# Four gate slabs beside the last dilated attention items, norm sums closed by one more matmul, and both directions of a linear attention interleaved

## The chip, the cores and the metric

One Trainium2 chip, one core. The metric is the device time of one execution in microseconds (us). The kernel is one program with five instruction streams: TensorE (PE), VectorE (DVE), ScalarE (ACT), GpSimd (POOL) and SyncE (SP, which only issues DMAs). They meet at semaphores.

## The reference, cut to what matters

Two transformer blocks run one after the other on 512 tokens of width 1024, with a context of 256 tokens beside the second. Everything is f32.

```
# first block
merged = sigmoid(gate_dn) * (o_dn @ w_branch_dn) + sigmoid(gate_da) * (o_da @ w_branch_da)
h = h + merged @ w_out            # o_dn: gated delta rule, o_da: dilated attention
# norm, used ten times
y = x * rsqrt(mean(x*x) + eps) * g
# linear attention (GLA) of the second block, for both directions
b = cumsum(log_sigmoid(z) / 16)                       # per chunk of 64 tokens
q_in, k_in, k_end = q * exp(b), k * exp(-b), k * exp(b_last - b)
a_intra = where(lower, q_in @ k_in.T, 0)
state_{c+1} = exp(b_last) * state_c + k_end.T @ v     # scan over the chunks
o = a_intra @ v + q_in @ state_c                      # then neighbourhood and window attention
```

The second block has two layers. Layer 0 runs the GLA for the context (c0) and for the latent tokens (l0), layer 1 needs only the context's final states (c1) and the latent tokens (l1).

## The kernel before, in words

**Slabs.** Each weight matrix is cut into slabs of 128 output features. A slab is loaded by SP into one of four raw buffers, split by ACT (`split_scalar`, L502) and DVE or POOL (`split_lower`, L510) into a high and a low part, and multiplied by TensorE in 24 matmuls of 512 columns (`unit_tensor`, L544, L546, L555): high by high, high by low, low by high. A slab of 512 tokens takes TensorE 5.44 us. The list `spine` fixes the order of all slabs.

**Side streams.** All work that is no slab (delta rule, dilated attention, GLA, attention) is written as generators, one for each engine. A planner (`Weave`) walks through the spine before the program is written, keeps a modelled clock for each engine, and puts the next step of a side stream between the matmuls of a slab when its model says that the operands will be there. What comes out is one static order for every engine. An engine that waits at the head of its order holds up all that was placed behind it. `drain` places the rest of a stream with no slab beside it.

**Dilated attention.** Four heads of four items each (`dilated_tensor`): scores (L1471 to L1473), softmax, six transposes (L1479), twelve matmuls with the values (L1491), a transpose back (L1497). The items of a head can start only after its last value slab. After the 36 slabs of the dilated projections come the four slabs z; then the stream is drained, the residual is loaded (`xres`, L1757), and the gates and merges follow.

**Norm sums.** ACT squares the eight blocks (`square_scalar`, L618), POOL adds the first seven (`sum_gpsimd`, L632), and TensorE sums over the partitions by a matmul with ones: one for POOL's sum (L638) and one for the eighth square (L640).

**GLA.** The generator `gla(m)` runs direction 0 from end to end and then direction 1. For each direction: decay matmuls (L1984) and their bias on DVE (L2152); Abs, Exp, Ln on ACT (L2085 to L2089); softplus, the two scans and the difference on DVE (L2156 to L2163); three or four Exp on ACT (L2096 to L2104); the products with keys and queries (L2169, L2173, L2238); key transposes (L2000); the states by chunk (L2013, mask L2183) and their scan (L2195); the entering states times the queries (L2031); scores inside the chunks and their product with the values (L2045, L2209, L2055). When direction 1 is done the event `mixed` lets the first lane of the neighbourhood attention begin; the output norm of the GLA (L2069, L2131 to L2139, L2218, L2221) gives the event `normed`, at which the second lane begins; a third lane begins after the last projection slab. In layer l the attention of 12 near items is then drained with what is left of the lanes, since the output slabs need its results. In the latent layers (`lat`), l0 stands for layer 0 and l1 for layer 1; 23 projection slabs run beside the GLA.

Of the kernel before, what the change touches and what calls it, by code (L numbers as in the profile page):

```python
# [15 lines left out]
T = 512  # L16
# [391 lines left out]
def program(nc, io):  # L408
# [215 lines left out]
    def sum_gpsimd(g, nm, use, c, before=None):  # L624
        g.wait_ge("sum_a", use, c)
        if c == 0:
            if before:
                g.wait_ge("sum_t", before)
            g.x.tensor_copy(nm.acc[:], nm.sq[0][:]).then_inc(*g.gives("sum_g", use, c))  # L629
        elif c < KC - 1:  # L630
            g.wait_ge("sum_g", use, c - 1)
            g.x.tensor_tensor(nm.acc[:], nm.acc[:], nm.sq[c % 2][:], ALU.add).then_inc(*g.gives("sum_g", use, c))  # L632

    def sum_tensor(t, nm, use):
        o = take(t, nm.ring, ("norm", use), ("norm_a", use, "ln"))[:, 0:nm.n]
# [4 lines left out]
        t.x.matmul(o, ones[:], nm.sq[(KC - 1) % 2][:], start=False, stop=True).then_inc(*t.gives("sum_t", use))  # L640
# [1058 lines left out]
    gate = [sb(f"gate{i}", WK + 82 + 2 * i, [T]) for i in range(6)]  # L1699
    mg_hi, mg_lo = sb("mg_hi", WK + 56, [KC, T], F32R), sb("mg_lo", WK + 98, [KC, T], F32R)  # L1700
    mg_pairs = [Pair(mg_hi[:, c], mg_lo[:, c], ("merge_a", c), ("merge_v", "lo", c)) for c in range(KC)]

    def gate_buffer(which, o):
        return gate[(2 * o + "dn da".split().index(which)) % 6]
# [91 lines left out]
    def ctxnorm_tensor(t):  # L1796
        for c in range(KC):
            yield 0.9
        yield coming("clate", ("sum_g", "c0mix", KC - 2), ("sum_a", "c0mix", KC - 1))
# [36 lines left out]
    class Mixer:  # L1836


        def __init__(self, name, l, v, n, base, full, pairs):
# [27 lines left out]
            self.dec = sb(f"{name}_dec", 8.5 if lat else 8.75, [2, self.NCH])  # L1867
# [79 lines left out]
    def gla(m):  # L1947
# [18 lines left out]

        def tensor(t):
            for i in range(2):
                yield When(("evac", place_of["proj", (m, "gv", i)], 0))
                yield coming(m.ring, m.there("gv", i))  # L1970
                b = take(t, m.ring, (name, "gv", i), ("gla_v", name, "gv", i))
                t.wait_ge(*m.there("gv", i))
                for o, s in zip(blocks(b), blocks(m.gvT[:, i])):
                    ins = t.x.transpose(o, s, ident)
                ins.then_inc(*t.gives("gla_t", name, "gv", i))
                yield 0.3
            yield When(("evac", place_of["proj", (m, "za", 0)], 0))
            for d in range(2):
# [8 lines left out]
                if d == 0:  # L1987
                    yield When(("evac", place_of["proj", (m, "gk", 1)], 0))
                    if full:
                        yield When(("evac", place_of["proj", (m, "gq", 1)], 0))  # L1990
                yield Ready(("gla_a", name, "soft", d))
                yield 0.3
                yield Ready(("gla_a", name, "past", d))
                yield 0.0
                yield coming(m.ring, ("gla_v", name, "kend", d), n=2)
# [7 lines left out]
                if d == 1 and full:  # L2003
                    yield Mark((name, "qk done"))
# [13 lines left out]
                if not full:  # L2018
                    continue
# [7 lines left out]
                for k, c in enumerate(chunks(d)):  # L2027
# [7 lines left out]
                    elif k % 2:  # L2035
                        yield 0.3
                for n0 in range(0, NT, 2):
# [22 lines left out]
                    yield 0.2  # L2060
            if not full:
# [13 lines left out]
        def scalar(a):  # L2075
            for i in range(2):
                yield
            for d in range(2):
                for i in range(2):
                    a.wait_ge("gla_v", name, "z", d, i)  # L2080
                if d:
                    a.wait_ge("gla_g", name, "kin", 0) if full else a.wait_ge("gla_v", name, "kend", 0)
                for f in m.idle:
                    a.wait_ge(*f)
                a.x.activation(m.C[:], m.tmp[:], ACT.Abs, bias=0.0, scale=1.0).then_inc(*a.gives("gla_a", name, "abs", d))  # L2085
                a.wait_ge("gla_a", name, "abs", d)
                a.x.activation(m.C[:], m.C[:], ACT.Exp, bias=0.0, scale=-1.0).then_inc(*a.gives("gla_a", name, "exp", d))
                a.wait_ge("gla_a", name, "exp", d)
                a.x.activation(m.C[:], m.C[:], ACT.Ln, bias=1.0, scale=1.0).then_inc(*a.gives("gla_a", name, "soft", d))  # L2089
                yield  # L2090
                C4 = m.C[:].rearrange("p i (c s) -> p i c s", s=64)
                for i in range(2):
                    a.wait_ge("gla_v", name, "scan", d, i)
                if d:
                    a.wait_ge("gla_v", name, "state", 0, NCH - 1, 1)
                a.x.activation(m.dec[:], C4[:, :, :, 63 if d == 0 else 0], ACT.Exp, bias=0.0, scale=-1.0 / 16).then_inc(  # L2096
                    *a.gives("gla_a", name, "dec", d))
                a.wait_ge("gla_v", name, "past", d)
                a.x.activation(m.tmp[:], m.tmp[:], ACT.Exp, bias=0.0, scale=1.0 / 16).then_inc(*a.gives("gla_a", name, "past", d))
                if full:  # L2100
                    if d:
                        a.wait_ge("gla_t", name, "mix", 0, NT - 2)
                    a.x.activation(m.kin[:], m.C[:], ACT.Exp, bias=0.0, scale=1.0 / 16).then_inc(*a.gives("gla_a", name, "kin", d))
                    a.x.activation(m.qin[:], m.C[:], ACT.Exp, bias=0.0, scale=-1.0 / 16).then_inc(*a.gives("gla_a", name, "qin", d))  # L2104
                yield
                yield
# [7 lines left out]
                for _ in groups:  # L2114
                    yield
                if full:
                    for k in range(NCH - 1):
                        if k % 2:
                            yield
                    for n0 in range(0, NT, 2):  # L2120
                        yield
                        yield
# [18 lines left out]
        def vector(v):  # L2141
            for i in range(2):
                v.wait_ge("gla_t", name, "gv", i)
# [2041 lines left out]
```

## Time and profile before

| | us |
|---|---|
| median of 3 runs | 4046.06 (4045.66 to 4049.22) |
| the profiled execution | 4052.06 |
| its span, first to last instruction | 4049.8 |
| TensorE busy in the span | 3809.7 |
| mean granted clock of TensorE, as a share of full speed | 0.971 |

A row of the timeline has the start, the length, the engine, the line of the kernel, the operation with out<-in, the number of instructions merged, and in square brackets the time that the engine sat idle before it and who released it. A row of the windows has the stretch, its length, busy time and number of instructions of PE, PE's weight loads, DVE, ACT and POOL, then the granted clock, the DMA share and GB/s.

### The profile page before, as it was taken

The page shows a single profiled execution, that of the slowest core. Times are in us where ns is not written, and L with a number is a line of the kernel's source. Part 1 is how long each engine was busy: PE and PEld are TensorE (multiplying, and loading weights), DVE is VectorE, ACT ScalarE, POOL GpSimd, SP SyncE. Part 2 cuts the span into 40 slices and gives each one's busy share as a digit, 9 for nine tenths or more (in the row PEclk, how much of TensorE's full clock was granted, in tenths as well). Part 3 has the DMA queues.
Part 4 walks back from the last instruction along what each step waited for, and adds up shares of the span by engine and source line. Part 5 has one row for each costly group of instructions (what it writes and reads, how often), then busy time and mean ns, then how long its engine had stood idle before and what let it go on. Part 6 is the DMA issues. An engine that isn't in the chain of part 4 may idle for free. (4 is left out here: it accounts for less than half of the span.)

```text
span 4049.8 us, 57241 instructions
## 1 busy us (share of the span) xinstructions
PE 3809.7 (94%) x23037; PEld 3306.3 (82%) x23037; DVE 2407.7 (59%) x4212; ACT 1633.0 (40%) x2618; POOL 789.6 (19%) x630
## 2 busy tenths in 40 slices
PE   8999989989897989999999999997999999789998
PEld 5787767677797879999999999775687877677887
DVE  6455332456899777777777777556643335664333
ACT  4523332344455763333333333526532234564222
POOL 0112000253215643222332221201000010101000
PEclk9999999999999999999999999998999999899999
DMA  5211334432354479888888886321234332102322
GB/s 206 68 44 43 106 125 177 169 106 86 107 170 156 171 249 309 275 289 273 285 274 294 275 288 210 113 67 49 71 119 140 125 135 79 60 30 83 99 94 78
DMA packets 209191, 617.28 MB, mean 152 GB/s; under 512 B 18464, under 2 KB 68640, under 8 KB 205088
## 3 DMA queue, kind: packets, MB, share of 16 engines
q1 hardware_dynamic: 168352, 465.76, 34.7%
q0 software_dynamic: 40576, 147.87, 10.3%
q8 instruction: 183, 3.00, 0.3%
q14 instruction: 80, 0.66, 0.0%
HBM read 583.67 MB, written 29.88 MB: 152 GB/s over the span
## 5 line engine op out<-in xcount | busy, mean ns | idle before, releaser
L510 DVE TENSOR_TENSOR wlo<-raw,whi 128x1024 fp32r<-128x1024 f32 x576 | 714.6, 1241 | 676.0 <-ACT whi L502 668.2
L544 PE MATMUL ps<-hhi,whi 128*128 128x512 f32 (+1 forms) x2824 | 1074.9, 381 | 13.2 <-ACT uact L3384 8.9
L546 PE MATMUL ps<-hlo,whi 128*128 128x512 f32 (+1 forms) x2824 | 1049.0, 371 | 0.4 <-DVE hlo L2609 0.4
L502 ACT ACTIVATE whi<-raw 128x1024 fp32r<-128x1024 f32 x660 | 694.7, 1054 | 622.1 <-PE ps L555 471.1
L555 PE MATMUL ps<-hhi,wlo 128*128 128x512 f32 (+1 forms) x2824 | 663.2, 373 | 0.0
L544 PEld LDWEIGHTS ps<-hhi,whi 128*128 128x128 f32 x2824 | 533.0, 189 | 116.2 <-issue 24.4
L546 PEld LDWEIGHTS ps<-hlo,whi 128*128 128x128 f32 x2824 | 533.2, 189 | 68.7 <-issue 3.6
L555 PEld LDWEIGHTS ps<-hhi,wlo 128*128 128x128 f32 x2824 | 511.4, 188 | 72.0 <-issue 4.8
L544 PE MATMUL ps<-ag_hi,whi 128*128 128x384 f32 x1024 | 342.1, 334 | 0.0
L546 PE MATMUL ps<-ag_lo,whi 128*128 128x384 f32 x1024 | 342.0, 334 | 0.0
L510 POOL TENSOR_TENSOR wlo<-raw,whi 128x1024 fp32r<-128x1024 f32 x85 | 210.4, 2484 | 184.2 <-ACT whi L502 183.5
L3500 POOL DMA_INDIRECT fetched<-peer_v_rows,rows x128 | 150.9, 1179 | 361.6 <-DVE xtok L3472 335.5
L3500 POOL DMA_INDIRECT fetched<-peer_u_rows,rows x128 | 153.3, 1198 | 338.5 <-DVE ract L3458 329.8
L3384 ACT ACTIVATE uact<-ps 128x384 f32<-128x384 f32 x128 | 63.0, 492 | 367.0 <-PE ps L555 367.0
L544 PE MATMUL ps<-hchi,whi 128*128 128x256 f32 x672 | 177.6, 298 | 33.3 <-ACT whi L502 21.4
L555 PE MATMUL ps<-ag_hi,wlo 128*128 128x384 f32 x1024 | 198.1, 334 | 0.0
L544 PEld LDWEIGHTS ps<-ag_hi,whi 128*128 128x128 f32 x1024 | 192.2, 188 | 0.0
L546 PEld LDWEIGHTS ps<-ag_lo,whi 128*128 128x128 f32 x1024 | 192.1, 188 | 0.0
L555 PEld LDWEIGHTS ps<-ag_hi,wlo 128*128 128x128 f32 x1024 | 179.4, 188 | 0.0
L546 PE MATMUL ps<-hclo,whi 128*128 128x256 f32 x672 | 172.3, 290 | 0.0
L3401 DVE TENSOR_TENSOR uact<-uact,gin 128x384 f32<-128x384 f32 x128 | 71.3, 557 | 163.9 <-ACT uact L3384 153.4
L629 POOL COPY nacc<-nsq 128x512 f32<-128x512 f32 x6 | 3.7, 610 | 820.6 <-ACT nsq L618 820.6
(630 smaller groups left out, 6303.3 us busy)
## 6 DMA issues: line engine op xcount, KB each, us to landing
raw<-w_in SPq DMA_DIRECT2D x151, 512.0 KB, 3.6
raw<-peer_u SPq DMA_DIRECT2D x128, 512.0 KB, 4.7
raw<-peer_v SPq DMA_DIRECT2D x128, 512.0 KB, 4.3
raw<-w_mod SPq DMA_DIRECT2D x96, 512.0 KB, 3.6
raw<-w_gate SPq DMA_DIRECT2D x66, 512.0 KB, 3.5
raw<-w_up SPq DMA_DIRECT2D x66, 512.0 KB, 3.5
raw<-w_down SPq DMA_DIRECT2D x66, 512.0 KB, 3.5
gate_dram<-stage SPq DMA_DIRECT2D x24, 1024.0 KB, 6.1
```

What stands on the lines that cost most here:

```text
L502: a.x.activation(whi[n % NW][:], raw[i % NRAW][:], ACT.Copy, bias=0.0, scale=1.0).then_inc(*a.gives("hi", i))
L510: e.x.tensor_tensor(wlo[n % NW][:], raw[i % NRAW][:], whi[n % NW][:].bitcast(F32), ALU.subtract).then_inc(*e.gives(*lo_sig(i)))
L544: t.x.matmul(o, w, p.hi, start=grp.opens and k == 0, stop=False)
L546: t.x.matmul(o, w, p.lo, start=False, stop=False)
L555: ins = t.x.matmul(o, lo[:, 128 * (starts[gi] + k):128 * (starts[gi] + k) + 128], p.hi, start=False, stop=grp.closes and k == len(grp.pair ...
L629: g.x.tensor_copy(nm.acc[:], nm.sq[0][:]).then_inc(*g.gives("sum_g", use, c))
L3384: a.x.activation(uact[j % 2][:], held(("out", "peer_u", j))[:, 0:TD], ACT.Gelu_apprx_tanh, bias=0.0, scale=1.0).then_inc(*a.gives("peer_a" ...
L3401: v.x.tensor_tensor(t3, t3, gin[g % 2][:, :, jj, :], ALU.mult).then_inc(*v.gives("peer_v", "gated", j))
L3500: g.x.indirect_dma_start(fetched[i % NF][:], None, io["peer_v_rows" if i >= 128 else "peer_u_rows"], bass.IndirectOffsetOnAxis(ap=rows[:, ...
```

## The change

Three edits. (1) The gate slabs dn and da of the first two output blocks stand before the z slabs instead of behind them. They get four buffers of their own, and their sigmoid waits for the last transpose of the delta rule's output. The spine runs eight slabs instead of four before the dilated stream is drained. (2) POOL adds six squares instead of seven; TensorE adds the seventh and the eighth by matmuls with ones. (3) `gla` is cut into named steps, and one order sets them for both directions: direction 1's decays, scans and key transposes are placed among the states and the entering part of direction 0. Direction 1 has its own decay buffer and works in the buffer of the value projections, free by then. The products of direction 1 with its queries and inner keys are still behind the mixing of direction 0.

```diff
-        elif c < KC - 1:
+        elif c < KC - 2:
             g.wait_ge("sum_g", use, c - 1)
             g.x.tensor_tensor(nm.acc[:], nm.acc[:], nm.sq[c % 2][:], ALU.add)...
-        t.wait_ge("sum_g", use, KC - 2)
+        t.wait_ge("sum_g", use, KC - 3)
         t.x.matmul(o, ones[:], nm.acc[:], start=True, stop=False)
-        t.wait_ge("sum_a", use, KC - 1)
-        t.x.matmul(o, ones[:], nm.sq[(KC - 1) % 2][:], start=False, stop=True)...
+        for c in (KC - 2, KC - 1):
+            t.wait_ge("sum_a", use, c)
+            ins = t.x.matmul(o, ones[:], nm.sq[c % 2][:], start=False, stop=c == KC - 1)
...
+    gate_first = [sb(f"gate_first{i}", WK + kb, [T]) for i, kb in enumerate((62, 64, 66, 60))]
...
-        if o >= 3:
+        if o < 2:
+            a.wait_ge("unit_t", 3)
+        elif o < 5:
+            a.wait_ge("da_v", "oda", 3, 3)
+        else:
             a.wait_ge("merge_v", "lo" if which == "dn" else "sum", o - 3)
-        else:
-            a.wait_ge("da_v", "oda", 3, 3)
...
+        decs, Cs = [m.dec, m.dec2], [m.C, m.gvT]
+        def order(values_by_token, gates, decays, ends, turning, sums, entered, mix, keys):
+            yield from values_by_token()
+            yield from gates(0)
+            yield from decays(0)
+            yield from keys(0)
+            yield from ends(0)
+            yield from turning(0)
+            yield from gates(1)
+            yield from sums(0)
+            yield from decays(1)
+            if full:
+                yield from entered(0)
+            yield from ends(1)
+            yield from turning(1)
+            if full:
+                yield from mix(0)
+            yield from keys(1)
+            yield from sums(1)
+            if full:
+                yield from entered(1)
+                yield from mix(1)
...
+                    if d and full and (c0, p) == groups[1]:
+                        queries(d)
...
-    spine += ... + coupled(u_da[-12:], m0[16:32]) + u_z + u_merge[:2]
-    spine += coupled(u_merge[2:] + u_out[:6], m0[32:] + m1[:16]) + u_out[6:]
+    spine += ... + coupled(u_da[-12:], m0[16:32]) + u_merge[:4] + u_z
+    spine += coupled(u_merge[4:] + u_out[:6], m0[32:] + m1[:16]) + u_out[6:]
...
     run(36)
-    run(4)
+    run(8)
     plan.drain("dilated")
     plan.put("do", "xres")
-    run(24)
+    run(20)
```

In the named steps, `gates` are the decay matmuls with Abs, Exp, Ln; `decays` softplus, scans and Exp; `keys` the two Exp for inner keys and queries; `ends` the product with the keys; `turning` the key transposes; `sums` the states and their scan; `entered` and `mix` the two parts of the output.

## Rows read from the trace of the kernel before

**Rows 1.** The page, part 1, TensorE.

```profile
PE 3809.7 (94%) x23037; PEld 3306.3 (82%) x23037; DVE 2407.7 (59%) x4212; ACT 1633.0 (40%) x2618; POOL 789.6 (19%) x630
```

**Rows 2.** Windows over the drained dilated items and the two latent layers.

```profile
577.00:598.00 21.00, 11.67 (x45) 8.94 (x45) 4.03 (x11) 7.66 (x12) 0.54 (x1) 0.59 0.35 119
2705.00:2750.00 45.00, 44.99 (x261) 36.43 (x260) 22.93 (x45) 18.26 (x28) 1.79 (x3) 1.00 0.15 48
2750.00:2800.00 50.00, 28.79 (x174) 20.12 (x173) 36.45 (x80) 33.22 (x65) 10.78 (x13) 0.69 0.21 67
2800.00:2830.00 30.00, 25.76 (x228) 20.39 (x224) 19.78 (x60) 18.50 (x40) 2.17 (x3) 0.90 0.09 28
3491.00:3541.00 50.00, 28.65 (x174) 19.90 (x172) 36.46 (x80) 33.16 (x65) 10.77 (x13) 0.68 0.21 67
3541.00:3571.00 30.00, 25.70 (x226) 20.47 (x226) 19.85 (x60) 18.50 (x40) 2.17 (x3) 0.90 0.09 27
```

**Rows 3.** Timeline of TensorE: scores of three dilated items, and the first gate slab.

```profile
560.97 1.02 PE L1471 MATMUL ps<-dk,dq 128*128 128x512 f32 x2
...
574.45 1.02 PE L1471 MATMUL ps<-dk,dq 128*128 128x512 f32 x2
...
587.09 2.07 PE L1471 MATMUL ps<-dk,dq 128*128 128x512 f32 x2 [0.47 <-DVE oda L1553]
...
597.99 0.47 PE L544 MATMUL ps<-hhi,whi 128*128 128x512 f32 x1
```

**Rows 4.** Timeline of ACT: one of six table loads between 550 and 588 us.

```profile
552.68 1.28 ACT L1590 ACT_TABLE_LOAD   x1
```

**Rows 5.** Timeline of SP: the loads of the residual.

```profile
580.89 3.65 SPq L1757 DMA_DIRECT2D xres<-xT  x8
```

**Rows 6.** Timeline of TensorE at two of the ten norm sums.

```profile
2927.27 1.13 PE L638 MATMUL ps<-nacc,ones 128*128 128x512 f32 x2 [1.19 <-POOL nacc L632]
...
3310.95 1.13 PE L640 MATMUL ps<-nsq,ones 128*128 128x512 f32 x2 [0.65 <-ACT nsq L618]
```

**Rows 7.** Timeline of TensorE: the GLA of l0, from the mixing of direction 0.

```profile
2664.41 1.09 PE L2055 MATMUL ps<-l_aT,l_gvtok 128*64 128x128 f32 x16
...
2692.23 1.03 PE L2000 MATMUL ps<-cst,l_tmp 128*128 128x128 f32 x8
...
2695.49 1.16 PE L2013 MATMUL ps<-l_gvtok,l_ktok 64*128 64x128 f32 x8
...
2711.11 0.55 PE L2031 MATMUL ps<-l_qin,l_S 128*128 128x64 f32 x4
...
2727.01 1.09 PE L2055 MATMUL ps<-l_aT,l_gvtok 128*64 128x128 f32 x16
```

**Rows 8.** Timeline of DVE in l0: scans of direction 1, end of the output norm.

```profile
2680.21 2.34 DVE L2160 TENSOR_TENSOR_SCAN l_C<-c,l_tmp 128x512 f32<-128x512 f32 x2
...
2747.02 0.75 DVE L2221 SCALAR_TENSOR_TENSOR l_tmp<-l_tmp,cst,l_gg 128x512 f32<-128x512 f32 x1
```

**Rows 9.** Timeline of ACT in l0: an Exp of direction 1.

```profile
2684.06 1.04 ACT L2099 ACTIVATE l_tmp<-l_tmp 128x1024 f32<-128x1024 f32 x1
```

**Rows 10.** Timeline of TensorE: near items of l0, and one item's transposes at full clock.

```profile
2735.59 0.36 PE L2396 MATMUL ps<-l_nks,l_nqd 128*128 128x256 f32 x1
...
2750.28 0.28 PE L2396 MATMUL ps<-l_nks,l_nqd 128*128 128x256 f32 x1
...
2761.92 0.55 PE L2396 MATMUL ps<-l_nks,l_nqd 128*128 128x256 f32 x1 [4.72 <-ACT l_nqd L2755]
...
2772.29 1.04 PE L2414 MATMUL ps<-cst,l_NS 128*128 128x128 f32 x8
...
2783.83 0.58 PE L2396 MATMUL ps<-l_nks,l_nqd 128*128 128x256 f32 x1 [5.35 <-DVE l_o L2515]
```

**Rows 11.** Timeline of TensorE: the longest GLA stalls of c0 and c1.

```profile
908.62 1.12 PE L2031 MATMUL ps<-c_qin,c_Sen 128*128 128x64 f32 x4 [2.76 <-DVE c_Sen L2195]
...
1432.01 0.63 PE L2000 MATMUL ps<-cst,c_tmp 128*128 128x128 f32 x4 [2.21 <-DVE c_tmp L2169]
```

More of the change, by code:

```diff
@@ L636, in sum_tensor @@
         t.wait_ge("ones_g")
-        t.wait_ge("sum_g", use, KC - 2)
+        t.wait_ge("sum_g", use, KC - 3)
         t.x.matmul(o, ones[:], nm.acc[:], start=True, stop=False)
-        t.wait_ge("sum_a", use, KC - 1)
-        t.x.matmul(o, ones[:], nm.sq[(KC - 1) % 2][:], start=False, stop=True).then_inc(*t.gives("sum_t", use))
+        for c in (KC - 2, KC - 1):
+            t.wait_ge("sum_a", use, c)
+            ins = t.x.matmul(o, ones[:], nm.sq[c % 2][:], start=False, stop=c == KC - 1)
+        ins.then_inc(*t.gives("sum_t", use))
     def root_scalar(a, nm, use, before=None, eps=EPS):
@@ L1703, in gate_buffer @@
     def gate_buffer(which, o):
-        return gate[(2 * o + "dn da".split().index(which)) % 6]
+        i = 2 * o + "dn da".split().index(which)
+        return gate[i % 6] if o >= 2 else gate_first[i]
     def gate_scalar(a, i, phase):
@@ new lines, in nothing, with steps, values_by_token, gates @@
+        def nothing(count):
+            def steps(*_):
+                for _ in range(count):
+                    yield
+            return steps
+        no_steps = {"values_by_token": nothing(2), "gates": nothing(1), "decays": nothing(1), "keys": nothing(0), "ends": nothing(1),
+                    "turning": nothing(1), "sums": nothing(len(groups)), "entered": nothing((NCH - 1) // 2), "mix": nothing(NT)}
+        def tensor(t):
+            def values_by_token():
+                for i in range(2):
+                    yield When(("evac", place_of["proj", (m, "gv", i)], 0))
+                    yield coming(m.ring, m.there("gv", i))
+                    b = take(t, m.ring, (name, "gv", i), ("gla_v", name, "gv", i))
+                    t.wait_ge(*m.there("gv", i))
+                    for o, s in zip(blocks(b), blocks(m.gvT[:, i])):
+                        ins = t.x.transpose(o, s, ident)
+                    ins.then_inc(*t.gives("gla_t", name, "gv", i))
+                    yield 0.3
+                yield When(("evac", place_of["proj", (m, "za", 0)], 0))
+            def gates(d):
@@ L2002, in tensor, with sums @@
                 yield 0.3
-                if d == 1 and full:
-                    yield Mark((name, "qk done"))
+            def sums(d):
                 for c0, p in groups:
@@ L2017, in tensor, with entered @@
                     yield 0.3
-                if not full:
-                    continue
+                if d == 1 and full:
+                    yield Mark((name, "qk done"))
+            def entered(d):
                 yield Ready(("gla_v", name, "qin", d), ("gla_v", name, "state", d, NCH - 2, 1),
@@ L2060, in tensor @@
                     yield 0.2
+            yield from order(**{**no_steps, "values_by_token": values_by_token, "gates": gates, "decays": decays, "ends": ends,
+                                "turning": turning, "sums": sums, "entered": entered, "mix": mix})
             if not full:
@@ L2113, in scalar @@
                 yield
[L2114 to L2122, printed above, removed]
+            yield from order(**{**no_steps, "gates": gates, "decays": decays, "keys": keys, "turning": turning})
             if not full:
@@ L2166, in vector, with ends @@
                 yield
+            def ends(d):
                 v.wait_ge("gla_a", name, "past", d)
@@ L2169, in vector, with queries, sums @@
                 v.x.tensor_tensor(m.tmp[:], m.tmp[:], m.gk[:], ALU.mult).then_inc(*v.gives("gla_v", name, "kend", d))
-                if full:
-                    v.wait_ge("gla_a", name, "qin", d)
-                    v.wait_ge(*m.there("gq", 1))
-                    v.x.tensor_tensor(m.qin[:], m.qin[:], m.gq[:], ALU.mult).then_inc(*v.gives("gla_v", name, "qin", d))
+                if full and d == 0:
+                    queries(d)
                 yield
-                yield
+            def queries(d):
+                v.wait_ge("gla_a", name, "qin", d)
+                v.wait_ge(*m.there("gq", 1))
+                v.x.tensor_tensor(m.qin[:], m.qin[:], m.gq[:], ALU.mult).then_inc(*v.gives("gla_v", name, "qin", d))
+            def sums(d):
                 if d:
@@ L2212, in vector @@
                     yield
+            yield from order(**{**no_steps, "values_by_token": values_by_token, "gates": gates, "decays": decays, "ends": ends,
+                                "sums": sums, "mix": mix})
             if not full:
@@ L2249, in gpsimd @@
                     g.x.tensor_copy(m.r_S[:, d], m.Sen[:, chunks(d)[-1]]).then_inc(*g.gives("gla_g", name, "final", d))
-                if not full:
-                    continue
-                for k in range(NCH - 1):
-                    if k % 2:
-                        yield
-                for n0 in range(0, NT, 2):
-                    yield
-                    yield
+            yield from order(**{**no_steps, "ends": ends, "sums": sums})
             if full:
```

109 lines of the change are left out of this document (52 added, 57 removed).

## The prediction, on record before the result was known

> **What bounds the kernel now.** I read the page first. TensorE is busy in 94% of the span [rows 1], so 4049.8 - 3809.7 = 240 us are all that waiting costs, beside what a lowered clock costs (mean clock 0.971). No edit here takes work off TensorE, and the second adds some. So a part of the change is worth what it removes of TensorE's idle time and of its time at the lower clock, and nothing else. The next view was the windows, over the whole span in slices of 50 us, to see where that time lies; three of the lowest stretches are next to the change [rows 2]. Between 577 and 598 us TensorE is busy for 11.67 us of 21, and the granted clock is 0.59: the reader is to see that even the busy time is stretched, since most of it runs at 1.2 GHz and not at 2.4. Behind each of the two latent layers' projections lie 80 us with 54.6 us busy at clocks of 0.69 and 0.90 (l0) and 54.4 us at 0.68 and 0.90 (l1). The 45 us before them are full: 44.99 us busy at 1.00. Last I read the timeline engine by engine in these stretches, to see what TensorE waits for and what had to come first.
>
> **The gate slabs.** The drained part of the dilated stream holds the end of one item and two whole ones, with scores at 574.45 and 587.09, and the first slab behind it starts at 597.99 [rows 3]. The work that TensorE has there is, at full clock, between 11.67 / 2 = 5.8 us (all of it was at half clock) and 11.67 x 0.59 = 6.9 us (busy time by mean clock) [rows 2]. So the stretch of 21 us loses 14.1 to 15.2 us. Four gate slabs, at 5.44 us each, are 21.8 us of TensorE work that is ready: they read only the normalised input. That is more than the hole. With cover, two items start 574.45 - 560.97 = 13.5 us apart [rows 3]. The item at 574.45 is the third of its head, so the first stands two of these steps ahead, near 548; four items need 3 x 13.5 from there and some 11 us to the end: 600. Eight slabs are 43.5 us, and with some 13 us of dilated work between them TensorE is full until about 605. The stream ends before the slabs do, and the whole loss goes: I take 14.5 us.
>
> Three things are queued anew. ACT changes its table for Sigmoid, Silu and Exp in turn; before, it did so six times in this part, at 1.28 us each [rows 4]. The new order has four more evacuations between the same four softmaxes, so at most two loads for each item, 2.6 us, of which an item had 1.28 or 2.56 before; the slack is (605 - 600) / 4 = 1.25 us an item, so it about fits. The residual's eight loads took 3.65 us to issue at 580.89, while TensorE waited anyway [rows 5]; now they are issued once z is gated, near 609, and the slab loads queued on SP stand behind them. Two slabs are split ahead and four more lie in the raw buffers, at least 11 us of work against about 4 us to wait and 4 us to issue, plus the bytes; I take 0, and 3 us as the bad end. The sigmoid waits for the delta rule's output, whose last part was done before 515 us by its place in the timeline: 0.
>
> The Trainium skill, in "ScalarE: Activation LUTs", "What ACT_TABLE_LOAD costs", gives about 1283 ns for a load and another 1380 ns of drain, 2.66 us for every switch, and in "Table sets: the hidden batching unit" asks for all work of one set before the next. It speaks against this edit, which mixes three sets. The trace agrees with the load (1.28 us) but shows no drain beside it: the activation behind the load of 552.68 starts as it ends, at 553.97. By the page's figure two switches an item would be 5.3 us, some 4 us over the pitch that I use, and the estimate for the gain would fall from 14.5 to 7 us.
>
> **The norm sums.** An extra matmul of 512 columns in f32 costs some 0.87 us at full clock (a pair of records starts about that far apart). Where POOL's last addition was waited for (1.19 us before L638 at 2927.27) the acc matmul can start 1.2 us sooner and is followed by one more: 1.19 - 0.87 = 0.3 us won, in l0 and again in l1. Where POOL was early and the last square came late (0.65 us before L640 at 3310.95) the extra matmul fills that wait and sticks out by 0.2 us; three sums look so [rows 6]. In the other five the sum lies beside slabs, at a low clock or behind a wait for ACT that stays. Together -0.3 us; both ends +-2 us.
>
> **The GLA.** In l0 direction 0 ends its mixing at 2665.5. Direction 1's key transposes come at 2692.23, its first states at 2695.49: 30 us in which only decays, scans and keys were made [rows 7]. In the new order these lie beside the states of direction 0. From the states on, direction 1 keeps what it had, 2695.49 to 2728.1. What is new before direction 0's mixing is a chain behind its state scan: softplus, two scans (2.34 us) and a difference, 4.8 us on DVE [rows 8]; a table load and an Exp of 1.04 us [rows 9]; the key product, 1.2 us; transposes (1.03 us) and their copy, 1.1 us. That is 11.5 us, of which the entering part hides 6 us: +5.5 us. The two Exp of `keys`(1) and the query product hide behind the first two state groups (2 x 2.2 us). So `mixed` comes 30 - 5.5 = 24 us earlier, at 2704 instead of 2728. TensorE's own work there is unchanged and was under full slabs, so this alone gives nothing. What counts is that the near attention starts under the slabs. Its first scores followed `mixed` by 7.5 us (2735.59); the second lane followed the end of the output norm (2747.8, 19.7 us after `mixed`) with scores at 2750.28 [rows 8, 10]. Now these come at 2711 and 2726, and the slabs, which ended at 2750, run to about 2762 because the attention's matmuls come between them. In the before, an item under slabs was slow: from 2735.59 its values were done near 2766, since its queue positions on DVE lay behind the output norm. Two lanes in 50 and 36 us get through 4 items by that measure (2 if each takes the 30 us seen, 6 if 14 us).
>
> The 80 us behind the slabs lose 80 - (28.79 x 0.69 + 25.76 x 0.90) = 37 us in l0 and the same in l1 [rows 2], for twelve items: 3.1 us an item. Four items fewer save 12.4 us. The stall of 4.72 us for the second set of operands [rows 10] goes too, since these follow the output norm and now fall under the slabs, and the 1.8 us of value copies beside it. Sum 18.9; I take 18 us a layer, 36 us for both. The bounds are 6 us a layer (two items, no stall gone: the like of the 5.35 us [rows 10] comes in its place) and 30 us (six items and both stalls). DVE has room for it: 22.93 us busy in the 45 us before [rows 2].
>
> In c0 the context attention begins only after the last slab, and TensorE is full there; in c1 the gate work of the experts follows at its own pace. An earlier GLA releases nobody. The stalls inside it, 2.76 and 2.21 us [rows 11], may go or be doubled by the new queue positions: I take -1 us, ends -5 and +5 us.
>
> **The sum.** 4052.06 - 14.5 - 0.3 - 36 - 1 = 4000.3 for an execution like the profiled one, which lies 2.3 us above its span and 6.0 us above the median of the runs. Against the median: 4046.06 - 51.8 = 3994 us.
>
> **The rivals.**
> (a) The near attention does not profit: earlier lanes sit behind other instructions in DVE's or ACT's fixed order, as the first item did for 30 us, and only as much as 0 to 4 us a layer is won. For it: that first item, and the third lane still waits for the last slab. Against: DVE is half idle there. Time 4046 - 15 - 4 = 4027.
> (b) The dilated items become slower than 14.75 us apart, by table loads or by the longer queue on ACT, and half or all of the first gain goes: 4001 to 4008.
> (c) The near attention gets nearly all of its 37 us back in both layers (six items or more and no new stall): 4046 - 15 - 66 - 3 = 3962.
> (d) The change moves the waits but not the end, all three parts: the slabs' order or the drains are bound by something that the profile puts down to another releaser: 4046.
> (e) On the other side: direction 1's decay steps stand early in the order of ACT and DVE, in front of slab splits. If TensorE runs out of split slabs (there are two, 10.9 us) because ACT waits there for DVE and DVE for the transposes, each latent layer and c0 pays 5.44 us or more and the attention behind it is not covered better. It decides from a loss of 14.5 / 2 = 7.3 us a layer on; at 12 us a layer the time is 4046 - 15 + 24 = 4055. Against: the same steps stood in the same queues before without a stall in 44.99 of 45 us.
>
> **How the numbers follow.** Forecast 0.62 (3966 to 4022), a 0.13, b 0.08, c 0.06, d 0.05, e 0.06. The low end is 4046 - 16 - 60 - 4 = 3966. The high end takes in a, with a bad end of the residual's loads and of c0: 4033. Outside are c in part, d and e, and together with the tail of a they are under 0.2. Within 0.2%, or 8 us, two times of this kernel can't be told apart. Faster by more than that: forecast, a, b, c, 0.89. Within: d, 0.05. Slower: e, 0.06.
>
> **What would show it.** Right: no idle hole of TensorE before `xres`, and 20 us less between the first z or gate slab and the first merge; the last L2055 of l0 some 24 us closer to its first L1974; near scores (L2396) for three or four items more before the last projection slab; less than 60 us from that slab to the last near item. Wrong: new idle time before L544 with whi as releaser in the GLA stages, or an unchanged distance from the last projection slab to the window attention.

## The result, and the profile after

The kernel after takes 4029.0 us (median of 5 runs, 4023.9 to 4035.6) against 4046.3 us: the ratio is 0.9956, 95% interval 0.9941 to 0.9970, so 17 us less and not the 52 us forecast. The profiled execution, the slowest of the five, has a span of 4033.8 us, 16.0 us under the 4049.8 us of before. Part 1 of its page:

```profile
PE 3813.2 (95%) x23057; PEld 3313.6 (82%) x23057; DVE 2406.4 (60%) x4212; ACT 1638.7 (41%) x2622; POOL 773.9 (19%) x620
```

**Where the 16 us come from.** The sums of the ten norms cut both programs at the same places. Between them the kernel after wins 9.2 us in the dilated stage, gate, merge and output slabs, 10.6 us in c0 with the context's attention, 1.5 us in l0 and 1.4 us in l1 (forecast 18 each); it loses 3.7 us between the context's two norms and 3 us in the stages not named here. The table of stages below has them for all kernels.

**Dilated items.** Windows of the kernel after, where [rows 2] has 577 to 598 us of before:

```profile
577.00:604.00 27.00, 27.00 (x140) 22.49 (x139) 10.93 (x20) 16.41 (x23) 0.54 (x1) 1.00 0.18 54
...
604.00:617.00 13.00, 8.84 (x42) 5.38 (x40) 2.04 (x3) 3.14 (x5) 0.00 (x0) 0.97 0.69 243
617.00:640.00 23.00, 21.96 (x92) 14.92 (x92) 6.86 (x8) 5.46 (x6) 0.00 (x0) 0.87 0.52 182
```

The hole is gone: 27.00 us busy of 27.00, clock 1.00. The next two rows are new: 4.16 + 1.04 us idle, and a mean clock of 0.87 in the second. That mean is 6.8 us at half clock (1.2 GHz) and full clock behind:

```profile
616.11:622.94 6.83, 4.90 (x11) 2.62 (x12) 2.45 (x2) 2.11 (x2) 0.00 (x0) 0.50 0.81 291
622.94:640.00 17.06, 17.06 (x82) 12.30 (x81) 4.41 (x6) 3.35 (x4) 0.00 (x0) 1.00 0.43 151
```

Timelines of TensorE and SP in the kernel after:

```profile
617.50 1.92 PE L827 MATMUL ps<-raw,svec 128*32 128x512 f32 x4 [4.66 <-DMA raw<-w_mod]
```

```profile
588.83 0.33 SPq L494 DMA_DIRECT2D raw<-w_mod  x1
606.64 3.65 SPq L1763 DMA_DIRECT2D xres<-xT  x8
610.33 0.46 SPq L494 DMA_DIRECT2D raw<-w_mod  x1
```

Between 588.83 and 610.33 SP issues no slab load: it stands at the residual's loads, which wait until z is gated, and TensorE runs out of loaded slabs.

**The latent layers.** TensorE in l0, kernel after. In [rows 7], counted from the first decay matmuls at 2598.43, direction 0 ended its mixing at 67.1 us and direction 1 at 129.7.

```profile
2582.69 1.10 PE L2026 MATMUL ps<-l_za,wa 128*128 128x512 f32 x2 [1.03 <-DVE l_gvtok L2195]
2615.68 1.36 PE L2048 MATMUL ps<-cst,l_tmp 128*128 128x128 f32 x8 [2.08 <-DVE l_tmp L2226]
2636.68 1.16 PE L2061 MATMUL ps<-l_gvtok,l_ktok 64*128 64x128 f32 x8
2649.19 0.50 PE L544 MATMUL ps<-hhi,whi 128*128 128x512 f32 x1 [2.12 <-DVE l_nk L1936]
2658.18 1.03 PE L2048 MATMUL ps<-cst,l_tmp 128*128 128x128 f32 x8
2670.50 1.09 PE L2107 MATMUL ps<-l_aT,l_gvtok 128*64 128x128 f32 x16
2672.65 1.16 PE L2061 MATMUL ps<-l_gvtok,l_ktok 64*128 64x128 f32 x8
2702.70 1.09 PE L2107 MATMUL ps<-l_aT,l_gvtok 128*64 128x128 f32 x16
2709.76 0.28 PE L2453 MATMUL ps<-l_nks,l_nqd 128*128 128x256 f32 x1
2714.99 0.86 PE L2764 MATMUL ps<-cst,l_nvT 128*128 128x128 f32 x4 [2.23 <-ACT l_C L2181]
2723.92 0.28 PE L2453 MATMUL ps<-l_nks,l_nqd 128*128 128x256 f32 x1
```

Counted from 2582.69, direction 0's last mixing (2670.50) ends at 88.9 us: 21.8 us later than before, where the prediction had 5.5. Direction 1's ends at 121.1: its part shrank from 62.6 to 32.2 us, as forecast, so `mixed` is 8.6 us earlier and not 24. And there are three waits of 2.1 to 2.2 us that were not there. Within 1.3 us behind each begins a stretch of 3.4 us at half clock; all the rest of the slab stretch is at full clock:

```profile
2616.32:2619.73 3.41, 3.41 (x11) 2.83 (x10) 1.49 (x2) 1.20 (x2) 0.00 (x0) 0.50 0.25 52
2650.45:2653.86 3.41, 3.41 (x14) 3.02 (x14) 2.71 (x3) 1.55 (x2) 0.00 (x0) 0.50 0.17 34
2715.30:2718.71 3.41, 3.41 (x14) 2.83 (x12) 0.85 (x2) 3.38 (x4) 0.00 (x0) 0.50 0.00 0
```

Windows of l0, the slab stretch from the first decay matmuls and the drained stretch behind it, first before, then after:

```profile
2598.40:2750.40 152.00, 150.38 (x794) 119.80 (x794) 78.51 (x115) 59.19 (x74) 8.48 (x9) 1.00 0.23 77
2750.40:2828.50 78.10, 52.65 (x389) 39.04 (x387) 55.72 (x138) 50.69 (x103) 12.95 (x16) 0.76 0.16 53
```

```profile
2582.70:2755.60 172.90, 165.90 (x878) 131.14 (x878) 99.96 (x159) 76.12 (x106) 15.80 (x17) 0.97 0.25 77
2755.60:2811.20 55.60, 36.21 (x303) 28.98 (x303) 37.27 (x95) 35.15 (x72) 5.82 (x8) 0.82 0.15 47
```

The drained stretch shrinks by 22.5 us, the slab stretch grows by 20.9. Of the 192 near value matmuls, all drained before, 32 (two items of twelve) now lie under the slabs, and the scores of two more items.

To weigh this, the loss is TensorE's idle time plus busy time times (1 - clock), summed over slices of 10 us. In l0, in us as idle + clock, for the slab stretch, the drained stretch and what follows up to the norm behind the attention:

| kernel | slabs | drained | to the norm |
|---|---|---|---|
| before | 1.6 + 0.0 | 25.4 + 11.2 | 7.1 + 0.0 |
| after | 7.0 + 4.1 | 19.4 + 5.2 | 5.9 + 1.4 |
| after, again | 7.2 + 1.3 | 19.4 + 3.7 | 5.8 + 2.9 |
| gates behind states | 6.0 + 2.7 | 16.2 + 6.4 | 5.8 + 0.0 |
| mixing first | 4.9 + 3.0 | 19.4 + 4.6 | 5.9 + 2.9 |
| GpSimd waits | 5.1 + 0.0 | 19.4 + 3.6 | 5.9 + 0.0 |
| three repairs | 3.9 + 1.7 | 16.8 + 6.7 | 5.8 + 1.4 |

The earlier attention saves 12.0 us of the drained loss (36.6 to 24.6), and the slab stretch gives 9.5 of it back (1.6 to 11.1).

### The profile page after: what moved, and what is told of

Same layout as the page of the kernel before. It is cut to its first block, busy times and chain, and to the rows that moved or that the text cites. A ratio compares the mean times of both kernels' runs of the same rounds, so it can differ in the third digit from the quotient of the medians.

```text
span 4033.8 us, 57266 instructions
## 1 busy us (share of the span) xinstructions
PE 3813.2 (95%) x23057; PEld 3313.6 (82%) x23057; DVE 2406.4 (60%) x4212; ACT 1638.7 (41%) x2622; POOL 773.9 (19%) x620
## 3 DMA queue, kind: packets, MB, share of 16 engines
q0 software_dynamic: 40576, 147.87, 10.4%
## 4 chain that ended last, share of the span: by engine, by line
PE 79%; DVE 11%; ACT 5%; DMA 2%; issue 2%; POOL 0%; SPq 0%; DVEq 0%; ACTq 0%; POOLq 0%
PE ps L544 22%; PE ps L546 21%; PE ps L555 21%; PE ps L2480 1%; PE ps L2453 1%; DMA raw<-w_in 1%; ACT whi L502 1%; PE ps L2471 1%; PE ps L827 1%; DVE hlo_plain L704 1%; PE ps L3351 1%; PE ps L2061 1%; DVE wlo L510 1%; DVE ea L3369 1%; DVE eb L3370 1%
```

## The experiments

Length of five stages in the profiled executions, in us: from the scores of the last head's first dilated item to the first latent norm sum; to the next context norm (c0 and its attention); to the one after; l0 and l1, each from the norm ahead of its projections to the norm behind its attention. The last columns are the median and the ratio to the kernel before, run beside each on its chip, with its interval.

| kernel | dilated to out | c0 | context | l0 | l1 | median | ratio |
|---|---|---|---|---|---|---|---|
| before | 258.0 | 280.1 | 289.2 | 354.2 | 359.4 | 4046.3 | 1 |
| after | 248.8 | 269.5 | 292.9 | 352.7 | 358.0 | 4029.0 | 0.9956 (0.9941, 0.9970) |
| gate slabs alone | 248.0 | 279.4 | 289.1 | 354.2 | 357.6 | 4040.0 | 0.9983 (0.9973, 0.9992) |
| norm sums alone | 257.0 | 278.0 | 292.3 | 353.1 | 357.6 | 4048.9 | 1.0002 (0.9993, 1.0011) |
| GLA order alone | 256.6 | 269.8 | 287.8 | 353.9 | 359.4 | 4039.9 | 0.9982 (0.9973, 0.9991) |
| after, old order in l0, l1 | 248.0 | 268.8 | 293.1 | 353.2 | 357.7 | 4034.4 | 0.9965 (0.9951, 0.9978) |
| residual later | 241.3 | 268.8 | 291.6 | 352.2 | 358.1 | 4021.5 | 0.9934 (0.9920, 0.9947) |
| mixing first | 249.1 | 268.3 | 291.7 | 348.6 | 353.8 | 4023.3 | 0.9936 (0.9922, 0.9950) |
| gates behind states | 251.3 | 268.8 | 291.8 | 347.0 | 353.3 | 4025.2 | 0.9941 (0.9927, 0.9955) |
| mixing first, all | 249.5 | 269.8 | 292.6 | 348.6 | 353.8 | 4025.9 | 0.9937 (0.9923, 0.9950) |
| after, again | 248.0 | 267.5 | 291.1 | 349.4 | 355.1 | 4030.4 | 0.9950 (0.9937, 0.9964) |
| GpSimd waits | 252.0 | 269.0 | 291.7 | 343.3 | 351.4 | 4025.1 | 0.9935 (0.9921, 0.9948) |
| two repairs | 240.9 | 268.8 | 291.8 | 347.0 | 353.3 | 4013.9 | 0.9907 (0.9891, 0.9922) |
| three repairs | 240.9 | 268.9 | 291.8 | 343.8 | 349.5 | 4007.9 | 0.9889 (0.9874, 0.9904) |

**Gate slabs alone.** Of the diff only the order of the slabs, their buffers and `run(8)`:

```diff
-    run(4)
+    run(8)
     plan.drain("dilated")
     plan.put("do", "xres")
```

> Only the four gate slabs ahead of the z slabs; norm sums and GLA as before. Theory A (read from the profile after): the hole of the drained dilated items goes (-14 us), but the residual's eight loads now stand ahead of the slab loads on SP until z is gated, TensorE waits about 5 us for a raw buffer near 617 us and runs some 3 us of work at a lower clock behind it; 8 us are left: 4038 us, with that wait in the trace. Rival B (the prediction's term, 14.5 us, is right and the loss of 5 us at 617 comes only together with the other edits): 4031.5 us, no wait for raw above 1 us near 617. Rival C: all 16 to 17 us of the change are this edit: 4029 us.

7 us by the ratio, 10.0 us in its stage, and the wait for raw is there (4.17 us at 614.60). Theory A; B's clean 14.5 us are not there, and C is out. The stage alone is a rough measure: it takes 248.0 to 252.0 us in the eight profiles that have this edit (and the residual's loads where they were), 256.6 to 258.0 us in the three that have not.

**Norm sums alone.**

```diff
-        elif c < KC - 1:
+        elif c < KC - 2:
```

> Only the seventh square summed by TensorE. Theory A: it moves waits and no time: 2.7 us won at the context norm near 1086 us (the wait for POOL's sum was 7.13 us), 3 us lost at the paired norms near 2567 us, where TensorE waits for two squares of ACT instead of one; others within 0.5 us each: 4046 us, within 2 us. Rival B: the prediction's 0.3 us with no such pair of larger terms: the same total, but the wait near 1086 us is still about 7 us.

No change, as both said, and by A's larger terms. Timeline of TensorE before, at the context norm and at the paired norms (two sums close together, near 2570 us):

```profile
1086.50 1.19 PE L638 MATMUL ps<-cnacc,ones 128*128 128x256 f32 x2 [7.13 <-POOL cnacc L632]
...
2567.76 2.04 PE L638 MATMUL ps<-chacc,ones 128*128 128x512 f32 x2 [3.96 <-POOL chacc L632]
2571.20 2.08 PE L640 MATMUL ps<-chsq,ones 128*128 128x512 f32 x2 [1.39 <-ACT chsq L618]
```

and with the norm edit alone:

```profile
1083.85 1.19 PE L638 MATMUL ps<-cnacc,ones 128*128 128x256 f32 x2 [4.41 <-POOL cnacc L632]
...
2565.91 1.12 PE L641 MATMUL ps<-chsq,ones 128*128 128x512 f32 x2 [1.69 <-ACT chsq L618]
2569.92 1.73 PE L641 MATMUL ps<-chsq,ones 128*128 128x512 f32 x2 [2.89 <-ACT chsq L618]
```

POOL's wait shrinks by 2.7 us at 1086, but the stage behind it grows by 3.1, and the first slab behind that norm starts at 1091.72 where it started at 1091.90; at the paired norms the wait of 3.96 us for POOL is gone, and two squares of ACT are waited for instead of one. The edit moved the wait from POOL to ACT.

**GLA order alone.**

```diff
+            yield from gates(1)
+            yield from sums(0)
+            yield from decays(1)
...
+            yield from ends(1)
+            yield from turning(1)
+            if full:
+                yield from mix(0)
```

> Only the new order of the two directions, in c0, c1, l0 and l1. Theory A (from the profile after): c0 gives 8 us, c1 nothing, each latent layer only 1.5 us, since direction 0's mixing ends 22 us later instead of 5.5: 4035 us. Rival B (the prediction): 18 us a latent layer and 1 us in the contexts: 4009 us. Rival C: the latent layers lose as much as c0 gives: 4046 us.

7 us by the ratio. c0 wins 10.3 us (280.1 to 269.8), l0 and l1 together 0.3. The long stage with c1 and the experts, which the table leaves out, grows from 1192.1 to 1196.0 us, mostly by the clock: in its first 200 us TensorE's idle time grows by 0.5 us only. Nearest to Theory A, with less from the latent layers, a loss with c1, and 4040 us instead of 4035. In c0 the order removed waits; before it had these in the timeline of TensorE, and this window:

```profile
859.82 0.39 PE L544 MATMUL ps<-hchi,whi 128*128 128x256 f32 x1 [3.49 <-ACT c_gg L1913]
889.52 0.38 PE L544 MATMUL ps<-hchi,whi 128*128 128x256 f32 x1 [1.43 <-ACT c_nvT L1913]
896.95 0.39 PE L544 MATMUL ps<-hchi,whi 128*128 128x256 f32 x1 [1.41 <-ACT c_res L1913]
```

```profile
900.00:945.00 45.00, 42.24 (x293) 38.64 (x292) 19.61 (x52) 17.31 (x28) 27.84 (x16) 0.92 0.42 129
```

and with the GLA order alone two waits and this window of the same slabs:

```profile
857.34 0.39 PE L544 MATMUL ps<-hchi,whi 128*128 128x256 f32 x1 [1.29 <-ACT c_gg L1914]
879.03 0.66 PE L2042 MATMUL ps<-cst,c_tmp 128*128 128x128 f32 x4 [1.66 <-DVE c_tmp L2220]
```

```profile
899.00:935.00 36.00, 36.00 (x266) 33.54 (x265) 11.93 (x43) 17.22 (x27) 23.66 (x11) 1.00 0.44 135
```

All of TensorE's waits from 800 to 1092 us fall from 32.6 to 26.9 us in sum, the 2.76 us of [rows 11] among them. Over nine windows of the stage the clock costs 4 to 5 us less: busy time at 0.92 became busy time at 1.00.

**The kernel after with the old order in l0 and l1.**

```diff
+    def gla(m):
+        return gla_new(m) if not m.lat else gla_old(m)
```

> The kernel after, with the old order of the GLA in l0 and l1 alone (c0 and c1 keep the new one). Theory A: the new order is worth 1.5 us in each latent layer, so taking it back costs 3 us against the kernel after: about 4032 us; the distance from the norm before l0 to the one before its feed-forward part grows by 1 to 2 us. Rival B (the prediction's 18 us a layer are there, and something else in the kernel after eats them): 4065 us. Rival C (the order costs time in the latent layers and the single profile hides it): under 4027 us.

The stages l0 and l1 are 353.2 and 357.7 us, within a microsecond of the first profile of the kernel after and 6.4 us in sum above its second one. By the ratios (0.9965 against 0.9956 and 0.9950) the old order costs 4 to 6 us, near Theory A's 3, but the intervals overlap, and l0 and l1 grew as A expected only against the second profile. The new order is worth 0 to 6 us for both layers; B's 36 us are out, C too.

**Residual later.**

```diff
     run(8)
     plan.drain("dilated")
+    run(6)
     plan.put("do", "xres")
-    run(20)
+    run(14)
```

> The kernel after with the residual's loads put behind six more slabs of the spine. Theory A: what eats the gate slabs' gain is the SP queue, on which the slab loads stand behind a wait for z; without it the wait for raw of 4.7 us near 617 us and the 3 us of low clock behind it go: 6 to 8 us faster than the kernel after, 4022 us. Rival B (the raw buffers themselves come free late, the residual's place does not matter): the wait stays, 4029 us. Rival C (the eight loads collide further on with slabs or are late for the first output slab): the wait turns up elsewhere between 640 and 800 us, 4029 us or more.

The stage falls from 248.8 to 241.3 us, no wait for raw is left, and the window behind the dilated items is full at full clock:

```profile
617.00:640.00 23.00, 23.00 (x108) 17.20 (x107) 7.15 (x8) 6.12 (x8) 0.00 (x0) 1.00 0.61 213
```

Theory A. With this the gate slabs give 16.7 us in their stage (258.0 to 241.3).

**Mixing first.** In l0 and l1:

```diff
-            yield from gates(1)
             yield from sums(0)
-            yield from decays(1)
+            yield from gates(1)
             if full:
                 yield from entered(0)
-            yield from ends(1)
-            yield from turning(1)
+            yield from decays(1)
             if full:
                 yield from mix(0)
+            yield from ends(1)
+            yield from turning(1)
```

> The kernel after; in l0 and l1 alone direction 1's gates come behind direction 0's states and its key product and transposes behind direction 0's mixing. Theory A (mixing of direction 0 was late because direction 1's gates, decays and transposes stood in front of it in every queue): the mixing of direction 0 ends 67 to 72 us after the first decay matmuls (89 in the kernel after), that of direction 1 at 100 to 106 us (121), two or three near items more lie under the slabs at 3 us each: 6 us a layer, 4017 us. Rival B (near attention under the slabs gives nothing, since what the drained stretch loses less the slab stretch loses more in waits and clock): direction 1 ends as early, the time is 4029 us. Rival C (the tail of direction 1 grows, since its decays have less cover): mixing of direction 1 at 115 us or later, 4029 us.

Direction 0's mixing ends at 80.5 us (not 67 to 72), direction 1's at 117.3 (not 100 to 106). As a mechanism A fell and C held: the head wins 8.4 us and the tail behind it gives 4.6 of them back. The time is not C's: l0 and l1 win 4.1 and 4.2 us against the first profile of the kernel after, 2.1 in sum against the second. The slab stretch loses 7.9 us instead of 11.1 (8.5 in the second profile). The median is 6 us lower than the kernel after's, and the intervals of the ratios overlap.

**Gates behind states.** In l0 and l1 only `gates(1)` and `sums(0)` change places.

> The kernel after; in l0 and l1 alone the gates of direction 1 come behind the states of direction 0 instead of ahead of them, all else as in the kernel after. Theory A: of the 22 us by which direction 0's mixing was late, the gates ahead of the states make 10 (seen at the end of the states: 54 us after the first decay matmuls instead of 43) and the decays and transposes ahead of the mixing the other 12; but Abs, Exp and Ln now lie behind the states and the decays wait for them, so the second part grows: direction 1's mixing ends 115 to 121 us after the first decay matmuls, time 4025 to 4029 us. Rival B: all 22 us come from the gates: direction 0's mixing back at 67 us, direction 1's near 100, 4017 us.

The states of direction 0 are back (the last group at 45.0 us instead of 54.0), its mixing ends at 86.8, direction 1's at 119.9. Theory A, and its surprise: with `mixed` only 1.2 us earlier than in the kernel after the two layers are 10.4 or 4.2 us shorter (by its two profiles). By the medians the gain is 4 to 5 us. The wait of 2.12 us for `l_nk` is gone, but the one for the output norm's logarithm grew from 2.23 to 3.38 us, so under the slabs only 1.0 us of idle time is won; the drained stretch wins 3.2. So the gain does not go by when the mixing ends; what shortens the drained stretch was not tested.

**Mixing first in c0 and c1 too.** The same order for all four.

> The order that mixes direction 0 first (gates behind the states, key product and transposes behind the mixing) in c0 and c1 too. Theory A: c0 keeps its gain of 10 us only if the two waits of 2.8 us and the low clock behind them stay away; with little work in c0 the decays of direction 1 have less cover than in the kernel after, so c0 gives back 2 to 5 us against it: 4020 to 4023 us. Rival B: c0 gains by any order that mixes the two directions: 4017 us, the same as the order in l0 and l1 alone.

c0 269.8 us instead of 268.3 (267.5 to 269.5 in the kernel after), ratio 0.9937 instead of 0.9936: Rival B's equality, though at 4025.9 us and not at 4017. c0 gains by either order.

**The kernel after, again.**

> The kernel after itself, on the chip of the three runs beside it, so that they can be compared with it and not only with the kernel before. All theories: 17 to 19 us faster than the kernel before.

As expected. Its profile is that of the fastest of its five executions; it has the same waits and another clock. Windows of l0:

```profile
2578.72:2748.89 170.17, 162.98 (x878) 128.46 (x878) 100.83 (x159) 75.89 (x106) 15.81 (x17) 0.99 0.24 78
2748.89:2803.13 54.24, 34.84 (x302) 27.70 (x303) 37.01 (x95) 35.15 (x72) 5.83 (x8) 0.84 0.14 48
```

Idle time is 7.0 us and 7.2 us, the clock's share 4.1 and 1.3 (3.4 us at half clock behind one of the three waits, at 2644.29, instead of behind all three): l0 took 352.7 us once and 349.4 once.

**GpSimd waits.** In the kernel after VectorE's key product and GpSimd's product run at once:

```profile
2612.14 3.40 DVE L2226 TENSOR_TENSOR l_tmp<-l_tmp,l_gk 128x1024 f32<-128x1024 f32 x1
```

```profile
2611.89 2.56 POOL L2300 TENSOR_TENSOR l_kin<-l_kin,l_gk 128x1024 f32<-128x1024 f32 x1 [43.12 <-ACT l_kin L2159]
```

```diff
+                if m.lat:
+                    g.wait_ge("gla_v", name, "kend", d)
                 g.wait_ge("gla_a", name, "kin", d)
```

> The kernel after; in l0 and l1 GpSimd's product for the inner keys waits until VectorE's key product is done. Theory A: these two run at once in the kernel after, VectorE's takes 3.40 us instead of 1.21, and the key transposes of direction 0 wait 2.1 us for it, behind which the clock is 0.95 for 36 us: the product is back at 1.2 us, the wait at 0.3 us or less, each latent layer 3 to 4 us shorter, 6 to 8 us less than the kernel after. Rival B (VectorE is late there for another reason, the product's length is only how the wait is recorded): the product still takes 3.4 us and nothing is won. Rival C (the wait goes, but the clock falls anyway): 2 us a layer, 4 us.

With the wait, on VectorE, GpSimd and TensorE:

```profile
2614.56 1.22 DVE L2226 TENSOR_TENSOR l_tmp<-l_tmp,l_gk 128x1024 f32<-128x1024 f32 x1
```

```profile
2615.85 3.32 POOL L2302 TENSOR_TENSOR l_kin<-l_kin,l_gk 128x1024 f32<-128x1024 f32 x1 [44.64 <-DVE l_tmp L2226]
```

```profile
2618.17 2.08 DVE L510 TENSOR_TENSOR wlo<-raw,whi 128x1024 fp32r<-128x1024 f32 x1 [1.26 <-ACT whi L502]
```

```profile
2615.92 1.06 PE L2048 MATMUL ps<-cst,l_tmp 128*128 128x128 f32 x8
```

The product is back at 1.22 us, the wait of 2.08 us gone, the slab stretch of l0 loses 5.1 us at a full clock, and the layers are 6.1 and 3.7 us shorter than in the run beside it. 5.3 us less in the median, between A's 6 to 8 and C's 4, with overlapping intervals; the mechanism is A's, since the clock did not fall. GpSimd's product now runs into VectorE's next ones: it takes 3.32 us, and the split behind it 2.08 instead of 1.2, where TensorE does not wait. The Trainium skill ("SBUF — State Buffer", section "SBUF: two separate sides") says that the port pair of VectorE and GpSimd is an exclusive lock: a VectorE operation with two inputs in SBUF waits until a reading GpSimd operation that began first is done. The trace agrees: GpSimd began 0.25 us earlier and ended at 2614.45, and VectorE's 1.2 us ended at 2615.54.

**Two and three repairs.** Residual later and gates behind states; and GpSimd's wait as well.

> The kernel after with the residual's loads behind six more slabs and, in l0 and l1, the gates of direction 1 behind the states of direction 0. Theory A: the two are in different stages and add up: 5 us and 10 us, 15 us less than the kernel after, ratio to the kernel before 0.992. Rival B (part of what each gave was the chip's spread): 8 us or less.

> The same with GpSimd's product behind VectorE's key product in l0 and l1 as well. Theory A: 6 to 8 us more than with two repairs: 22 us less than the kernel after, ratio to the kernel before 0.990. Rival B: the later inner keys of direction 0 hold up its mixing, and the two are equal.

16.6 us and 22.5 us less than the kernel after beside them: Theory A both times, with 5.9 us from the third repair for the 6 to 8 expected. With all three the ratio to the kernel before is 0.9889 (0.9874 to 0.9904), 43 us by the medians. This version beats both kernels.

## Why the prediction was wrong

**Gate slabs, forecast 14.5 us, measured 7 (by the ratio) to 10.** The size of the hole was about right: the stretch is full, and with the residual's loads moved the stage gives 16.7 us. The step that failed is "I take 0" for the residual's loads. The 11 us of work ahead of the wait were counted from when z is gated, but SP had stopped at 588.83, 18 us before; the raw buffers were used up meanwhile. The bad end was 3 us, measured are 7.5 (248.8 less 241.3), since the idle 5.2 us also brought 6.8 us at half clock.

**Table loads.** Rival (b), slower items, came true for one step of three: the last one between items is 16.2 us, not the 13.5 of [rows 3]. TensorE did not wait before those scores (they stand behind slab matmuls in its order), so that the table loads made them late is not shown. The stream's last transpose was at 602.18 (forecast: 600) with slabs still under way, so it cost nothing. The drain that the Trainium skill gives ("ScalarE: Activation LUTs", "What ACT_TABLE_LOAD costs") is not seen this time either; timeline of ACT, kernel after:

```profile
578.15 1.28 ACT L1719 ACT_TABLE_LOAD   x1
579.45 0.60 ACT L1719 ACTIVATE gate_first<-ps 128x512 f32<-128x512 f32 x1
```

**Norm sums, forecast -0.3 us, measured 0 within 0.1% (4 us).** The sum agrees by luck. The prediction had POOL waited for in l0 and l1 only; TensorE also waited 7.13 us for it at 1086 and 3.96 us at the paired norms, and what the edit won there it lost right behind, in waits for ACT and the extra matmul.

**GLA in l0 and l1, forecast 36 us, measured 0 to 6.** Three steps failed. First, "+5.5 us" for the chain ahead of direction 0's mixing: measured 21.8. It priced the operations of direction 1 that stand there, but not what queues behind them. By the timeline 5.1 us come ahead of the first states, where the key product is held up by GpSimd and direction 1's decay matmuls and VectorE's part of the gates stand; with GpSimd's wait the first states come 3.8 us earlier (2.3 against the second profile), and direction 0's mixing ends at 83.5 us instead of 88.9 (87.3). 5.5 more come before the last group of states (43.4 us before, 54.0 after), where ACT works through three activations and their table loads before it reaches an evacuation and the next split; the other 11.2 lie between there and `mix(0)`, which stands behind direction 1's decays and key transposes. Timeline of ACT, first activation of direction 1's gates and first evacuation behind them:

```profile
2623.71 1.06 ACT L2138 ACTIVATE l_gvT<-l_tmp 128x1024 f32<-128x1024 f32 x1 [6.04 <-DVE l_tmp L2204]
...
2630.82 0.60 ACT L1920 ACTIVATE l_gg<-ps 128x512 f32<-128x512 f32 x1
```

Moving the gates alone brought the last states back by 9.0 us, which shows that part, but the mixing by 2.1 only, since the gates now stand between the two. Putting the mixing first as well won 6.3 us more of the 21.8 (86.8 to 80.5), and the tail grew by 3.7; how the remaining 13.4 us against before divide, no run told. Second, "Two lanes in 50 and 36 us get through 4 items": the first scores stand 46 and 32 us ahead of the slabs' end (2709.76 and 2723.92 against 2755.6), nearly the room forecast (51 and 36), because the slab stretch itself grew; but two items were finished in it. At the prediction's 3.1 us an item they and the two waits that went as forecast (4.72 and 1.75 us) make 12.7 us; measured are 12.0 instead of 18. Third, the slab stretch was priced at nothing for its new waits ("is unchanged and was under full slabs"): three waits of 2.1 to 2.2 us and the half clock behind them cost 9.5 us of the 12.0 us saved (6.9 of 13.5 in the second profile). Two of them are shown one by one: `l_nk` evacuated on VectorE behind `decays(1)`, gone when the gates moved, and the key product held up by GpSimd, gone with its wait. The third, 2.23 us for the output norm's logarithm, stayed in every variant of the new order (3.38 with the gates moved); no run tried it.

What held: two items finished under the slabs and two begun, DVE with room. Of the signs named, the hole is gone and 55.6 us lie behind the last slab (under 60), but the last mixing is 8.6 us nearer and not 24. Rival (a), 4027 us, came closest in time but by another way, which is luck: the attention did profit, and the slabs paid for it. Rival (e) named this kind of blocking. At 9.5 us a layer it is past the 7.3 us from which it was to decide; it did not, since that rival had the attention covered no better, and the attention gained 12.

**Contexts, forecast 1 us, measured 10 in c0, less 1 to 4 with c1.** "I take -1 us" for c0's stalls left out the clock behind them, and saw the GLA's stalls alone and not the evacuations held up behind its steps on ACT: before, `c_gg` stood behind four activations of the GLA, and TensorE waited 3.49 us for it; in the new order two of the four come behind it, and the wait is 1.29. Ends of 5 us either way were too narrow for c0. Its gain is more than half of the 17 us.

**The range.** The high end of 4033 leaves out 2 us of its own terms (4027 + 3 + 5 = 4035). The measured 4029 lies in it only because c0's gain made up for part of what the latent layers did not give.

## What to carry to other kernels

Before a step is moved ahead on one in-order queue, list what is then queued behind its waits on every engine, the DMA queue first, and price each item by what TensorE finds missing. A wait under otherwise full work can cost more than its length: behind the waits of 2.1 to 2.2 us here came 3.4 us at half clock, each time in one execution and once of three in another. So a stretch at 1.00 is worth protecting as much as a hole is worth filling. An earlier result is worth only what it releases: count which items really move before paying for it.

## What the hardware showed unexpectedly

- VectorE's product of 128x1024 took 3.40 us beside a GpSimd product begun 0.25 us earlier, and 1.22 us alone; with VectorE's begun first, GpSimd's took 3.32 us, against 2.40 in the kernel before.
- The same program with the same waits (7.0 and 7.2 us in l0) had a clock of 0.97 in one execution and 0.99 in another over the same slabs. Behind waits of 2.1 to 2.2 us the clock fell to 1.2 GHz for 3.4 us three times of three, and one time of three. What the waits cost was 11.1 us once and 8.5 us once, so a layer's stage read from one profile is good to 3 us only.
- Near a wait of 4.66 us the clock was at 1.2 GHz for 6.83 us (616.11 to 622.94), from 1.4 us before the wait's end to 5.4 us behind it, and at 2.4 GHz again from there on.
